# Recurrent gates of a two-block transformer: one true f32 product against three products of high and low parts

## The reference, cut to what matters

```python
def rg_lru(u, w_a, b_a, w_i, b_i, lam, reverse):
    r_gate = jax.nn.sigmoid(block_diag_linear(u, w_a, b_a))
    i_gate = jax.nn.sigmoid(block_diag_linear(u, w_i, b_i))
    log_a = -LRU_C * r_gate * jax.nn.softplus(-lam)
    a = jnp.exp(log_a)
    mult = jnp.sqrt(jnp.maximum(-jnp.expm1(2.0 * log_a), 0.0))
    bx = mult * (i_gate * u)
    _, h = lax.associative_scan(combine, (a, bx), axis=1, reverse=reverse)   # h = a * h_before + bx
u = centred_depthwise_conv(u, conv_w, conv_b)
y_rec = ((h_fwd + h_bwd) * jax.nn.gelu(y_branch)) @ w_rec_o
```

## Time and profile before

| | us |
|---|---|
| median of three runs | 3062.18 (3059.52 to 3063.20) |
| span of the profiled execution, first to last instruction | 3054.3 |
| median less that span | 7.9 |
| TensorE busy | 3001.5 (98%) |
| VectorE busy | 1968.5 (64%) |
| GpSimd busy | 1394.9 (46%) |
| ScalarE busy | 1046.4 (34%) |

### The profile page before, as it was taken

How to read it: one execution, slowest core, us unless ns; L and a number is a source line. 1 busy time by engine, 2 the same in 40 slices (tenths; PEclk the granted TensorE clock), 3 DMA queues, 4 the chain that set the end, 5 groups by cost and what they waited for, 6 DMA issues and landing times.

```text
span 3054.3 us, 38762 instructions
## 1 busy us (share of the span) xinstructions
PE 3001.5 (98%) x14552; PEld 2374.8 (78%) x14552; DVE 1968.5 (64%) x1900; ACT 1046.4 (34%) x1450; POOL 1394.9 (46%) x1100
## 2 busy tenths in 40 slices
PE   9999999998999999999999999999999999999998
PEld 7776668875878888888877777887678788888886
DVE  8989874435476777776656656121766766777764
ACT  3005773114243423322253534112652434323221
POOL 3433323330355667773323333333333556767760
PEclk9999999999999999999999999999999999999999
DMA  3111002130113423222212121422231224332331
GB/s 144 48 42 34 2 29 83 48 131 1 48 63 111 141 103 115 104 97 97 110 66 74 61 76 55 165 74 76 105 116 50 69 99 143 104 113 101 111 111 55
DMA packets 76917, 257.59 MB, mean 84 GB/s; under 512 B 7520, under 2 KB 8160, under 8 KB 74464
## 3 DMA queue, kind: packets, MB, share of 16 engines
q1 hardware_dynamic: 57696, 183.96, 17.9%
q10 hardware_dynamic: 19072, 71.60, 6.2%
HBM read 202.58 MB, written 52.95 MB: 84 GB/s over the span
## 4 chain that ended last, share of the span: by engine, by line
PE 85%; DVE 9%; ACT 2%; DMA 2%; issue 1%; POOL 1%; ACTq 0%; SPq 0%; DVEq 0%; POOLq 0%
PE psum L594 47%; PE psum L875 15%; PE psum L926 6%; PE psum L1100 3%; DVE cacc L1704 2%; PE psum L726 2%; PE psum L711 2%; PE psum L974 2%; PE psum L697 2%; DMA raw<-weights 1%; PE psum L1036 1%; PE psum L1050 1%; PE psum L1023 1%; DVE SX L1952 1%; PE psum L841 1%
## 5 line engine op out<-in xcount | busy, mean ns | idle before, releaser
L459 POOL TENSOR_TENSOR small<-par 128x1 f32<-128x1 f32 x168 | 44.8, 266 | 1137.2 <-PE psum L594 979.1
L594 PE MATMUL psum<-A_hi,w_hi 128*128 128x512 f32 x1536 | 481.7, 395 | 2.7 <-POOL w_lo L471 1.3
L594 PE MATMUL psum<-A_lo,w_hi 128*128 128x512 f32 x1536 | 473.3, 389 | 0.0
L594 PE MATMUL psum<-A_hi,w_lo 128*128 128x512 f32 x1536 | 472.9, 389 | 0.0
L465 POOL TENSOR_TENSOR w_lo<-raw,w_hi 128x1024 fp32r<-128x1024 f32 (+1 forms) x152 | 386.8, 2545 | 12.7
L594 PEld LDWEIGHTS psum<-A_hi,w_hi 128*128 128x128 f32 x1536 | 287.1, 188 | 72.8 <-issue 12.4
L594 PEld LDWEIGHTS psum<-A_hi,w_lo 128*128 128x128 f32 x1536 | 288.3, 188 | 60.3
L594 PEld LDWEIGHTS psum<-A_lo,w_hi 128*128 128x128 f32 x1536 | 288.3, 188 | 60.3
L594 PE MATMUL psum<-B_hi,w_hi 128*128 128x512 f32 x832 | 257.9, 391 | 1.1 <-DVE B_lo L2164 1.0
L594 PE MATMUL psum<-B_hi,w_lo 128*128 128x512 f32 x832 | 256.1, 389 | 0.0
L594 PE MATMUL psum<-B_lo,w_hi 128*128 128x512 f32 x768 | 236.6, 389 | 0.0
(11 more groups left out here) (338 smaller groups left out, 5626.0 us busy)
## 6 DMA issues: line engine op xcount, KB each, us to landing
raw<-weights SPq DMA_DIRECT2D x256, 512.0 KB, 3.3
hid<-TT ACTq DMA_DIRECT2D x60, 512.0 KB, 2.7
XSF<-hid SPq DMA_DIRECT2D x48, 512.0 KB, 5.1
gate_spill<-RU SPq DMA_DIRECT2D x16, 512.0 KB, 3.1
ULF<-hid SPq DMA_DIRECT2D x6, 1024.0 KB, 7.8
x_spill<-H ACTq DMA_DIRECT2D x1, 4096.0 KB, 11.1
R<-gate_spill ACTq DMA_DIRECT2D x8, 512.0 KB, 4.8
BE<-rel_bias ACTq DMA_DIRECT2D x8, 512.0 KB, 4.6
```

The source lines that it names most:

```text
L594: last = pe.matmul(PJ[s][:, c:c + step], w[:, s, k, :], b[:, k, c:c + step], start=(k == 0 and i == 0), stop=(k == kblocks - 1 and i == 2))
```

## The change

The gates become three passes like the other products. `WG` has one slot. GpSimd rounds it into `WGH` (the other half of the old pair) and writes the low part `WGL` over `WG` in place, so the load of the next gate weights waits on SP for all four gates of the round before (`r_gates`). VectorE copies the convolved input rounded into `RUH` (storage of `Z_[1]`) and subtracts into `RUL` (storage of `RC`); the subtraction now counts up `r_conv`. GpSimd's splits of the rounds are written out so that the gate weights are split behind the two splits of a round's first pair. TensorE's loop turns once per round instead of once per two.

```diff
@@ -218,7 +218,9 @@
         R_ = [at(f"R{i}", o_h + KIB4 * (1 + i), [SEQ]) for i in range(2)]
         I_ = [at(f"I{i}", o_h + KIB4 * (3 + i), [SEQ]) for i in range(2)]
         Z_ = [at(f"Z{i}", o_h + KIB4 * (5 + i), [SEQ]) for i in range(2)]
-        WG = [at(f"WG{i}", o_h + KIB4 * 7 + 2048 * i, [4, P]) for i in range(2)]
+        WG = at("WG", o_h + KIB4 * 7, [4, P])
+        WGH, WGL = at("WGH", o_h + KIB4 * 7 + 2048, [4, P], F32R), at("WGL", o_h + KIB4 * 7, [4, P], F32R)
+        RUL, RUH = at("RUL", o_h, [SEQ], F32R), at("RUH", o_h + KIB4 * 6, [SEQ], F32R)
         MIX, GA = at("MIX", o_a, [KB, SEQ]), at("GA", o_a + 32768, [KB, SEQ])
...
@@ -395,8 +397,8 @@
                 sp.wait_ge(free[s], 2 * m + (r0 + 2))
                 sp.dma_start(block_of(io["gate_spill"], m + KB * s), RC[:]).then_inc(S[f"g_out{s}"], 16)
-            def load_gates(m, slot):
-                sp.dma_start(WG[slot][:].rearrange("p a b -> p (a b)"), io["w_gates"][m]).then_inc(S[f"wg{slot}"], 16)
+            def load_gates(m):
+                sp.dma_start(WG[:].rearrange("p a b -> p (a b)"), io["w_gates"][m]).then_inc(S["wg"], 16)
             r0 = ROUNDS["rec_in"]
             for m in range(2):
@@ -410,13 +412,14 @@
                 load_round(r0 + 2 * m + 1, 1)
                 if m == 0:
                     sp.wait_ge(S["spilled"], 16)
-                    for slot in range(2):
-                        load_gates(slot, slot)
+                    load_gates(0)
+                    sp.wait_ge(S["r_gates"], 4)
+                    load_gates(1)
             with sp.Fori(1, 4) as i:
                 for par_ in range(2):
                     m = 2 * i + par_
-                    sp.wait_ge(S["r_gates"], 4 * m - 4)
-                    load_gates(m, par_)
+                    sp.wait_ge(S["r_gates"], 4 * m)
+                    load_gates(m)
                     for s in range(2):
                         load_round(2 * m + r0, s)
                     spill_gate(m - 1, 0)
@@ -547,7 +550,28 @@
             split(ROUNDS["ff"], 0)
             split(ROUNDS["ff"], 1)
             split_units("ff", 0, len(FF_UNITS))
-            splits(ROUNDS["rec_in"], ROUNDS["qkv2"] + 6)
+            def gate_split(m):
+                pool.wait_ge(S["wg"], 16 * m + 16)
+                if not (isinstance(m, int) and m == 0):
+                    pool.wait_ge(S["r_gates"], 4 * m)
+                pool.tensor_tensor(small[:, 12:13], par[:, 0:1], par[:, 0:1], ALU.mult)
+                chain(pool.tensor_scalar(WGH[:], WG[:], 1.0, 1.0, ALU.mult, ALU.mult))
+                pool.tensor_tensor(WGL[:], WG[:], f32(WGH[:]), ALU.subtract).then_inc(S["wg_split"], 1)
+            for s in range(2):
+                split(ROUNDS["rec_in"], s)
+            for s in range(2):
+                split(ROUNDS["rec_in"] + 1, s)
+            gate_split(0)
+            with loop(pool, 1, KB, {chain: 5}) as m:
+                for s in range(2):
+                    split(2 * m + ROUNDS["rec_in"], s)
+                gate_split(m)
+                for s in range(2):
+                    split(2 * m + (ROUNDS["rec_in"] + 1), s)
+            splits(ROUNDS["rec_out"], ROUNDS["qkv2"] + 6)
             split(ROUNDS["att_out"], 0, kb=4)
             for p in range(PAIRS):
@@ -952,7 +976,7 @@
             mlp("ff", A, B, 2, 0)
-            def rec_round(m, slot, first=False):
+            def rec_round(m, first=False):
                 q = 2 * m + ROUNDS["rec_in"]
                 if first:
                     job(q, 0, A, ready=norm_ready(3), order=[0, 1, 2, 3, 4, 5])
@@ -964,27 +988,25 @@
                 if first:
                     job(q + 1, 0, A)
                 pe.wait_ge(S["r_conv"], m + 1)
-                pe.wait_ge(S[f"wg{slot}"], (m // 2 + 1) * 16 if isinstance(m, int) else wg_value)
+                pe.wait_ge(S["wg_split"], m + 1)
                 for d in range(2):
                     for g in range(2):
                         if d or not first:
                             pe.wait_ge(S["r_sig"], 4 * m + (2 * d + g - 1))
-                        for h in range(2):
-                            last = pe.matmul(PX[:, 1024 * g + HALF * h:1024 * g + HALF * h + HALF],
-                                             WG[slot][:, 2 * d + g, :], RU[:, HALF * h:HALF * h + HALF],
-                                             start=True, stop=True)
+                        for i, (w, x) in enumerate(((WGH, RUH), (WGH, RUL), (WGL, RUH))):
+                            for h in range(2):
+                                last = pe.matmul(PX[:, 1024 * g + HALF * h:1024 * g + HALF * h + HALF],
+                                                 w[:, 2 * d + g, :], x[:, HALF * h:HALF * h + HALF],
+                                                 start=(i == 0), stop=(i == 2))
                         last.then_inc(S["r_gates"], 1)
                 if not first:
                     job(q + 1, 0, A)
                 job(q + 1, 1, A)
-            rec_round(0, 0, first=True)
-            rec_round(1, 1)
-            with pe.Fori(1, 4) as i:
-                wg_value = 16 * i + 16
-                rec_round(2 * i, 0)
-                rec_round(2 * i + 1, 1)
+            rec_round(0, first=True)
+            with pe.Fori(1, KB) as m:
+                rec_round(m)
             rounds("rec_out", 4, B, ready=(S["r_lo"], [k + 1 for k in range(KB)]))
@@ -2156,8 +2178,9 @@
                     if j == 2:
                         chain(dve.tensor_scalar(RU[:], RC[:], w, pcol("rec_conv_b", m), ALU.mult, ALU.add))
                     else:
-                        done = tl["r_conv"] if j == 3 else chain
-                        done(dve.scalar_tensor_tensor(RU[:, a:b], RC[:, a + j - 2:b + j - 2], w, RU[:, a:b], ALU.mult, ALU.add))
+                        chain(dve.scalar_tensor_tensor(RU[:, a:b], RC[:, a + j - 2:b + j - 2], w, RU[:, a:b], ALU.mult, ALU.add))
+                chain(dve.tensor_copy(RUH[:], RU[:]))
+                tl["r_conv"](dve.tensor_tensor(RUL[:], RU[:], f32(RUH[:]), ALU.subtract))
             def rec_out_lo(m):
                 dve.wait_ge(S["r_hi"], m + 1)
...
```

More of the change, by code:

```diff
@@ L262, in build @@
                  "u_hi u_sq u_lo st_hi st_sum st_lo st_weights st_done st_read hid0 hid1 hx_a hx_b hx_c hx_d sx_in us_split pair_sums pair_hi us_done us_copied us_read us_left us_right spilled std_out std_in "
-                 "wg0 wg1 r_conv r_scan r_gates r_sig r_z r_sq r_root r_y r_out r_hi r_lo "
+                 "wg wg_split r_conv r_scan r_gates r_sig r_z r_sq r_root r_y r_out r_hi r_lo "
                  "g_sig g_out0 g_out1 g_in0 g_in1 mixed_out0 mixed_out1 mixed_in gates_in att_sum split_hi split_lo x_back2 "
@@ L2198, in _ @@
             rec_block(0, first=True)
-            rec_per = {chain: 2 + 3 + 4, tl["r_conv"]: 1, tl["r_sq"]: 2, tl["r_scan"]: 2, tl["r_out"]: 1, tl["r_lo"]: 1}
+            rec_per = {chain: 2 + 3 + 6, tl["r_conv"]: 1, tl["r_sq"]: 2, tl["r_scan"]: 2, tl["r_out"]: 1, tl["r_lo"]: 1}
             with loop(dve, 1, KB - 1, rec_per) as m:
```

## The result

| | before | after |
|---|---|---|
| median (11 runs each) | 3058.98 | 3064.69 |
| span of the profiled execution | 3054.3 | 3062.6 |
| TensorE busy | 3001.5 | 2997.5 |
| VectorE busy | 1968.5 | 1989.6 |
| GpSimd busy | 1394.9 | 1429.2 |

The change makes the kernel slower by 5.7 us: the ratio is 1.0020, with an interval of 1.0011 to 1.0028 (3.4 to 8.6 us). The forecast was +11.7 and 3073.9, and its range began at 3066.0; the sign was right, the size twice too large. Of the 9.2 us by which the time was missed, 6.0 are the change; the other 3.2 are the base, since the median of three runs from which the forecast started (3062.18) lies 3.2 above that of eleven. Against its own base the range began at +3.8, so the change of +5.7 lies inside it; the time fell out of it by the base.

A forecast was written before the change was run, and what follows sets the result against it. TensorE was taken as the bound, with a VectorE chain 1% shorter that the change makes longer: six rounds +10.3, first interval +2.5, tail -1.1, total +11.7 us, forecast 3073.9, range 3066 to 3082.

The forecast's parts named there:

- The bound: TensorE's own work needs 49.30 us a round; the chain through the other engines, 52.07 after the change, sets it.
- TensorE's gates and the sigmoids: Three-pass gates take 5.77 us instead of 6.87; the last sigmoid ends at 7.40 instead of 8.50, giving the chain 1.12 back.
- The copy and the subtraction: On VectorE behind the last tap: two gaps of 0.15, copy 0.69, subtraction 1.22, together 2.21 us on the chain.
- Collision (a): GpSimd's rounding of the gate weights, behind VectorE's sum, holds up VectorE's product: 0.35 us on the chain.
- Collision (b): Behind the taps, GpSimd's rounding after the round's last job goes first and holds VectorE's new subtraction: 0.77 us a round.
- Rival A: VectorE's copy and subtraction win the lock against GpSimd: rounds of 50.95 to 51.35, total +4 to +8 us; chance 0.22.
- The first interval: The interval ahead of the six rounds, 40.9 us before, grows by 2.5 us, between +1.1 and +4.2.
- The moved steps at nothing: Later weight loads on SP, the gate split on GpSimd, its semaphore and TensorE's one-round loop cost nothing.
- a sign of being wrong: The forecast would be wrong if something waited for the gate weights or for a weight tile.
- The tail: Behind the last gates, with no new VectorE work, B_lo comes 1.12 earlier and TensorE's jobs end 1.10 earlier: -1.1 us.
- The clock: A wait of 2.8 us ahead of each round's gates leaves TensorE's clock unchanged.
- Rival D: The stall per round lowers TensorE's clock; the wait ahead of the gates absorbs most: 0 to 10 us more; chance 0.04.

The follow-up runs named there:

- experiment 1: Changed kernel without the copy and subtraction; the last tap writes the reduced type, all passes read it (product not the reference's): 3054.42 us, ratio 0.9986 to before.
- Experiment 2: Changed kernel with gates as true f32 matmuls again, copy, subtraction and weight split kept, low weights unused: 3073.47 us, ratio 1.0049 to before.
- experiment 9: Changed kernel with GpSimd's gate split moved to after VectorE's B_lo, where VectorE is idle: 3061.33 us, ratio 1.0008 to before.
- experiment 5: Changed kernel with one extra one-column VectorE instruction (about 0.2 us) ahead of the copy: 3068.16 us, ratio 1.0032 to before.
- 6: Changed kernel with two extra one-column VectorE instructions (0.4 us) ahead of the copy: 3078.23 us, ratio 1.0058 to before.
- experiment 3: Changed kernel with GpSimd splitting the gate weights ahead of a round's first tile instead of behind the second: 3064.04 us, ratio 1.0020 to before.
- experiment 7: Changed kernel with SP loading the second round's two weight tiles before it waits for the first round's gates: 3069.85 us, ratio 1.0032 to before.
- experiment 4: Changed kernel with TensorE starting gates on the copy alone and multiplying the low input part in the third pass: 3057.36 us, ratio 0.9996 to before.

## Why the prediction was wrong, by its steps

**The bound.** Right: TensorE's side 49.26 against a forecast of 49.30 (experiment 1), the chain above it, and the chain sets the round in after. (The two places of the earlier trace rows lie in two jobs, not in one, since 90 matmuls are more than a job's 48; the 0.2267 us stands.)

**TensorE's gates and the sigmoids.** Right. The third gate starts 2.98 us after the first (forecast 3.05), the last sigmoid ends 7.28 after it (7.40). Experiment 2 shows the 1.1 on the chain by itself.

**The copy and the subtraction.** Durations right: 0.69 and 1.23. The two gaps of 0.15 were wrong: they are 0.04 and 0.03. I took them from the row ahead of the last taps, where the profile names the tap before as releaser, and called them the price of a semaphore wait. The scan and the sum of the earlier trace rows stood in the same group and say otherwise: the scan ends at 1756.63 and the sum, which needs it, starts at 1756.66. Nor is it the taps as such. The taps ahead of the loop, in the first interval of after, take columns of `par` too, and stand 0.04 apart:

```profile
1570.53 3.92 DVE L2181 SCALAR_TENSOR_TENSOR TT<-RU,par,TT 128x1022 f32<-128x1022 f32 x3
```

Three taps of 1.28 are 3.84, which leaves 0.08 for two gaps; inside the loop, where the column is chosen by the loop's counter, the same gaps are 0.15 to 0.17. That points to the counter. No run changes it alone, so the cause stays open.

**Collision (a).** Right to the hundredth, 1.58 against 1.23, and by experiment 9 worth it (50.95 to 50.62 on average over the six rounds).

**Collision (b): the step that failed.** The forecast said that "The subtraction on VectorE asks at 50.08" and GpSimd's rounding comes before it, 0.77 us. The subtraction came first in all six rounds: in the round from 1730.45 it asked 49.48 us after the gates' start, and GpSimd's first instruction started at 49.69. In the round from 1730.45 the account is: 52.12 - 0.77 for (b) - 0.23 for the gaps - 0.27 for the DMA behind the take (3.29 instead of 3.56) - 0.10 for the sigmoids (8.50 to 7.28 is 1.22, not the 1.12 taken) + 0.09 to start TensorE = 50.84, as measured. Over six rounds the forecast was 10.3 and 3.4 came. Of the 6.9, (b) is 4.6 and the gaps 1.4. The mechanism, price and place of (b) were right, as experiments 5 and 6 show; which side gets the lock was wrong. The Trainium skill, "SBUF — State Buffer", "SBUF: two separate sides", says that whichever of the two operations starts first gets the port pair for the whole instruction; the eight meetings of this instruction in after agree, two lost and six won, and the prediction had used only the half of that rule that says how long the loser waits. The price hung on a margin that I had put at 0.25 us (49.83 against 50.08), of which the two gaps were 0.23. With the gaps right the copy would have ended at 49.82, 0.01 ahead of GpSimd's first instruction at 49.83, and the subtraction would have asked at 49.85. The rounding stands 0.15 behind that first instruction (1627.13 to 1627.28 in after), a step that the forecast left out; at 49.98 it would have been too late, so the forecast's own times then give the round to the subtraction. Rival A named this weakness, and its 50.95 to 51.35 a round and +4 to +8 in all are what came, at the lower end of its rounds. To give (b) 0.59 and its absence 0.22 was the fault of judgement.

**The first interval.** Forecast +2.5 between +1.1 and +4.2, came +3.2. Its cause was half seen, and the closeness of the sum is in part luck. The subtraction is held there, by 0.87 (2.09 us), by a rounding that began 0.02 us sooner; the rest was not added up. Experiments 3, 7 and 9, which leave its work as it is and only move when it is done, have it at 42.75, 46.54 and 42.16.

**The moved steps at nothing.** Right for the rounds: nobody waits for a gate weight there. In the first interval one tile came late (GpSimd waited 12.5 us for it), which the forecast had named as a sign of being wrong; experiment 7, where it is on time, has a longer interval, so no net loss by it is shown.

**The tail.** -1.2 against -1.1.

**The clock.** "That wait leaves TensorE's clock alone, I expect": right in after's profiled execution (1.00 throughout the stretch), wrong as a rule. Experiments 2, 3, 5, 6 and 7 each have one or two rounds that are 1.5 to 1.8 us longer than their neighbours (in experiment 5 with a lost meeting of about 0.9 on top, 2.4 in all), with a granted clock under 1.00 behind the stall ahead of the gates. Weight loads of experiment 3 at its round of 52.47, and its windows:

```profile
1628.48 0.39 PEld L999 LDWEIGHTS psum<-RUH,WGH 128*128 128x128 f32 x2 [3.06 <-issue]
1628.96 0.76 PEld L999 LDWEIGHTS psum<-RUL,WGH 128*128 128x128 f32 x2
1629.82 0.76 PEld L999 LDWEIGHTS psum<-RUH,WGL 128*128 128x128 f32 x2
```

```profile
1620.00:1630.00 10.00, 7.36 (x30) 5.74 (x29) 8.79 (x8) 0.00 (x0) 3.92 (x3) 0.93 0.00 0
1630.00:1640.00 10.00, 10.00 (x41) 7.85 (x40) 2.48 (x4) 5.54 (x5) 1.59 (x3) 0.90 0.24 86
```

The gates run at 1.2 GHz for some us, and they are on the chain, so it is paid in full. Rival D had the stall absorb it; a stall ahead of the gates can't, since it is over when they run. In after only the first interval has stalls as long as those that were followed by a fall (2.9 and 3.1 us; the rounds have 1.7 to 2.0). How often that costs its timed runs something, its one profile doesn't show.

## What to carry to other kernels

A term that exists only if one engine asks for a port before another is not a term but a fork: work out the margin, and where it is below the errors of the chain that leads up to it (here 0.2 us), give both sides their time and near-equal chances. Ask for each side what it waits behind: here GpSimd's place was decided while the copy ran, ahead of the subtraction that paid for it. A gap between dependent instructions is read from a pair of the same kind, not from the nearest wait of the same engine. When a chain and a bound lie 1% apart, order the new work so that the consumer waits for its first part only (experiment 4: 1.0 us a round), and put added GpSimd work where VectorE is idle (9: 0.3); together these turned +5.7 into -4.3 us.

## What the runs showed of the hardware

- Starting 0.02 us sooner is enough to have the lock: at 1575.21 (after), 1626.26 (experiment 3), 1730.88 (5) and 1733.75 (6) VectorE's subtraction started 0.02 behind GpSimd's rounding and took 2.09 or 2.10 instead of 1.23. The 0.02 comes from the copy ahead of both: GpSimd's work that started 0.13 us or more before the copy's end went first in 13 of 13 meetings, at 0.08 or less before it in none of 56. It works the other way too: GpSimd's one-column instruction took 1.07 instead of 0.19.
- A stall of the same length in the same place (2.24 and 2.25 us) was followed by the full clock in one execution and by half of it in another. In the stretches of all twelve profiles together, none of 50 stalls of TensorE (idle time ahead of a weight load) between 1.1 and 2.04 us was followed by a fall, and 10 of the 23 between 2.24 and 7.17 us were. A stall ahead of the work that the chain waits for is paid a second time in this way, 1.5 to 1.8 us.
- A rounding copy of 128x1024 on VectorE takes 0.69 us, as long as a copy that leaves the type.
